# Two-model kernel, odd layer: retention beside the value and gate chunks, output rows by readiness, rotations in pairs, final norm by quarter

## The reference

```python
h = rms_norm_2(x, norm_g)
rq, rk, rv, rz, eq, ez = _split(h @ w_in, ODD_SPLITS)      # 1024, 1024, 2048, 2048, 256, 256 columns
q = apply_rotary(rq, rcos, rsin); k = apply_rotary(rk, rcos, rsin) * 256 ** -0.5     # 4 heads of 256
r_out = head_group_norm(retention(q, k, v))                # per head: (q k^T * decay) v, 512 wide, then (o - mean) / std
m_out = memory_attention(eq, mem_n, w_mem_kv)              # 4 heads of 64 over 256 memory rows
y = concatenate([r_out * silu(rz), m_out * silu(ez)]) @ w_out                        # 2304 rows
x = x + y
return rms_norm_2(x, final_norm_g)
```

## Time and profile before

| | |
|---|---|
| median of 3 runs | 2457.4 us |
| profiled execution | 2458.76 us |
| its span | 2456.9 us |
| TensorE busy | 2359.7 us (96%) |
| VectorE busy | 1742.9 us (71%) |
| ScalarE busy | 1350.2 us (55%) |
| mean granted TensorE clock | 0.987 |

### The profile page before, as it was taken

The page is one execution under the profiler, slowest core; times in us unless marked ns, Lnnn a source line. Parts: engine busy times, 40 slices in busy tenths (PEclk is TensorE's granted clock), DMA queues, the critical chain, the costliest instruction groups (busy, mean ns, idle before and its releaser), DMA issues.

```text
span 2456.9 us, 45173 instructions
## 1 busy us (share of the span) xinstructions
PE 2359.7 (96%) x15676; PEld 2112.0 (86%) x15676; DVE 1742.9 (71%) x3162; ACT 1350.2 (55%) x2520; POOL 42.0 (2%) x86
## 2 busy tenths in 40 slices
PE   8999999999999999899999999999999989998988
PEld 7889998999988888899999899988888867776866
DVE  4656998999755555675999899856556667765464
ACT  4545555777554545445444677645555536744533
POOL 1000000000000000000000000000000000000010
PEclk9999999999999999999999999999999999999999
DMA  6344555444566666455556444566665642344533
GB/s 227 121 143 151 179 171 163 147 139 144 170 193 195 190 194 191 145 179 173 179 170 174 144 143 143 170 194 190 212 187 176 190 122 83 95 159 138 159 110 120
DMA packets 136825, 397.45 MB, mean 162 GB/s; under 512 B 12304, under 2 KB 13520, under 8 KB 135920
## 3 DMA queue, kind: packets, MB, share of 16 engines
q1 hardware_dynamic: 134144, 384.97, 51.9%
q0 software_dynamic: 2544, 10.67, 1.3%
HBM read 394.54 MB, written 1.05 MB: 161 GB/s over the span
## 4 chain that ended last, share of the span: by engine, by line
PE 69%; DVE 24%; issue 4%; ACT 2%; POOL 0%; DMA 0%; DVEq 0%; ACTq 0%; POOLq 0%; SPq 0%
PE bank L968 28%; PE bank L952 14%; PE bank L838 11%; DVE wl L1582 8%; PE bank L844 7%; PE bank L981 4%; DVE arena L1786 1%; DVE arena L1787 1%; DVE arena L1789 1%; DVE arena L1788 1%; PE bank L905 1%; PE bank L893 1%; ACT wh L1233 1%; PE bank L878 1%; DVE arena L1785 1%
## 5 line engine op out<-in xcount | busy, mean ns | idle before, releaser
L1582 DVE TENSOR_TENSOR wl<-raw,wh 128x1024 fp32r<-128x1024 f32 (+1 forms) x732 | 893.8, 1222 | 516.1 <-ACT wh L1233 502.3
L1233 ACT ACTIVATE wh<-raw 128x1024 fp32r<-128x1024 f32 (+1 forms) x732 | 771.7, 1055 | 643.5 <-PE bank L968 340.1
L952 PE MATMUL bank<-xh,wh 128*128 128x256 f32 x2048 | 512.4, 288 | 0.0
L952 PE MATMUL bank<-xl,wh 128*128 128x256 f32 x2048 | 501.7, 283 | 0.0
L952 PEld LDWEIGHTS bank<-xh,wh 128*128 128x128 f32 x2048 | 392.0, 191 | 1.3 <-issue 0.2
L952 PEld LDWEIGHTS bank<-xl,wh 128*128 128x128 f32 x2048 | 392.8, 192 | 0.0
L952 PE MATMUL bank<-xh,wl 128*128 128x256 f32 x2048 | 293.2, 286 | 13.3 <-DVE wl L1582 13.3
L952 PEld LDWEIGHTS bank<-xh,wl 128*128 128x128 f32 x2048 | 262.8, 191 | 20.8 <-DVE wl L1582 19.2
L968 PE MATMUL bank<-wh,gl 128*128 128x512 f32 x1024 | 274.4, 390 | 1.7 <-DVE gl L1908 1.7
L968 PE MATMUL bank<-wh,gh 128*128 128x512 f32 x1024 | 274.1, 389 | 0.5 <-ACT gh L1391 0.5
L968 PE MATMUL bank<-wl,gh 128*128 128x512 f32 x1024 | 273.8, 389 | 0.0
(11 more groups left out here) (279 smaller groups left out, 2737.5 us busy)
## 6 DMA issues: line engine op xcount, KB each, us to landing
raw<-in_w_upT SPq DMA_DIRECT2D x256, 512.0 KB, 3.6
raw<-in_w_down SPq DMA_DIRECT2D x256, 512.0 KB, 4.3
raw<-in_l_w_in SPq DMA_DIRECT2D x84, 512.0 KB, 3.6
raw<-in_peer_w_query SPq DMA_DIRECT2D x32, 512.0 KB, 3.8
raw<-in_l_w_out SPq DMA_DIRECT2D x28, 512.0 KB, 3.7
raw<-in_attn_w_qkv SPq DMA_DIRECT2D x24, 512.0 KB, 4.3
raw<-in_conv_w_in SPq DMA_DIRECT2D x24, 512.0 KB, 3.8
arena<-in_na_bias POOLq DMA_DIRECT2D x4, 1024.0 KB, 5.9
```

The costliest lines, as they stand in the source:

```text
L952: last = pe.matmul(banks[b][:, 0:SEQ], lhsT=w[part][:, k, :], rhs=x_in[xp][:, k, :], start=(k == 0 and part == 0 and xp == 0), stop=(k == ...
L1233: act.activation(wh[:, n % SPLIT, 0:kts * cols], raw[:, n % RAW, 0:kts * cols], ACT.Copy)\
L1582: tt(wl[:, n % SPLIT, 0:kts * cols], raw[:, n % RAW, 0:kts * cols], wh[:, n % SPLIT, 0:kts * cols].bitcast(F32), ALU.subtract).then_inc(lo ...
```

## The change

The plan is rewritten. Rotations come in pairs, at (c, 3) and (c + 1, 0), and their transposes three units behind the second; the memory attention starts one unit later; a head's `ret_S` and `ret_O` follow when its value chunk is there, so they lie beside the chunks of values and gates. `ret_O` writes the normalised output over the values and no longer multiplies by the gate; a new kind `z` does that for both tiles when `silu` is done. The transposes of the gated output (`zT`) and their split (`z_low`) move into the plan, in the order `ODD_YT`, and the rows of `odd_out`'s weights follow that order; groups 6 and 7 come after the second unit of `odd_out`. The low half of the gated output gets a place of its own in the arena. In the last unit all products of the first bank come before those of the second, and VectorE is told between. ScalarE squares the first two quarters between the units of `odd_out`'s second half. Each quarter is multiplied by gain and sqrt(1024) into `final` as soon as it is added; the row scale is applied by VectorE to the first column half and by ScalarE to the second; the output goes out in four stores of 256 KB.

```diff
 ODD_PLAN = {
     (0, 0): [("turn", 2)],
-    (0, 3): [("rope", 0)], (1, 1): [("rope", 1)], (1, 2): [("odd_T", 0), ("odd_T", 1)],
-    (1, 3): [("rope", 2)], (2, 1): [("rope", 3)], (2, 2): [("odd_T", 2), ("odd_T", 3)],
-    (2, 3): [("rope", 4)], (3, 1): [("rope", 5)], (3, 2): [("odd_T", 4), ("odd_T", 5)],
-    (3, 3): [("rope", 6)], (4, 1): [("rope", 7)], (4, 2): [("odd_T", 6), ("odd_T", 7)],
-    (4, 3): [("silu", 4), ("odd_T", 8)],
-    (8, 1): [("ret_S", 0)],
-    (9, 3): [("silu", 0), ("ret_S", 1)], (10, 0): [("ret_O", 0)],
-    (10, 3): [("silu", 1), ("ret_S", 2)], (11, 0): [("ret_O", 1)],
-    (11, 3): [("silu", 2), ("ret_S", 3)], (12, 0): [("ret_O", 2)],
-    (12, 3): [("silu", 3), ("ret_O", 3)],
+    (0, 3): [("rope", 0)], (1, 0): [("rope", 1)], (1, 3): [("odd_T", 0), ("odd_T", 1), ("rope", 2)],
+    (2, 0): [("rope", 3)], (2, 3): [("odd_T", 2), ("odd_T", 3), ("rope", 4)],
+    (3, 0): [("rope", 5)], (3, 3): [("odd_T", 4), ("odd_T", 5), ("rope", 6)],
+    (4, 0): [("rope", 7)], (4, 3): [("odd_T", 6), ("odd_T", 7), ("silu", 4)],
+    (5, 0): [("odd_T", 8), ("ret_S", 0)],
+    (6, 1): [("ret_O", 0)], (6, 2): [("ret_S", 1)],
+    (7, 1): [("ret_O", 1)], (7, 2): [("ret_S", 2)], (7, 3): [("mem_z", 0)],
+    (8, 0): [("zT", 0)], (8, 1): [("ret_O", 2), ("z_low", 0)], (8, 2): [("ret_S", 3)],
+    (9, 1): [("ret_O", 3)], (9, 3): [("silu", 0)],
+    (10, 0): [("z", 0)], (10, 2): [("zT", 1), ("zT", 2)], (10, 3): [("z_low", 1), ("z_low", 2), ("silu", 1)],
+    (11, 0): [("z", 1)], (11, 2): [("zT", 3), ("zT", 4)], (11, 3): [("z_low", 3), ("z_low", 4), ("silu", 2)],
+    (12, 0): [("z", 2)], (12, 2): [("zT", 5), ("zT", 6)], (12, 3): [("z_low", 5), ("z_low", 6), ("silu", 3)],
+    (13, 0): [("z", 3), ("ahead", 2), ("z_low", 7), ("z_low", 8)],
 }
+ODD_YT = (8, 0, 1, 2, 3, 4, 5, 6, 7)
+ODD_LATE = {1: (7, 8)}
...
-    ODD_PLAN.setdefault((5 + _s // 4, _s % 4), []).append(("om", _s))
+    ODD_PLAN.setdefault((5 + (_s + 1) // 4, (_s + 1) % 4), []).append(("om", _s))
...
-        weight("odd_out", d["l1_w_out_2"], D)
+        weight("odd_out", d["l1_w_out_2"], D, rows=ODD_YT)
...
+            for n in range(2):
+                for ready, k in ((final_ready, n), (final_scaled, 2 + n)):
+                    c, t = k // 2, k % 2
+                    sp.wait_ge(ready, n + 1)
+                    sp.dma_start(out[t * P:(t + 1) * P, c * CHUNK:(c + 1) * CHUNK], final[:, t, c * CHUNK:(c + 1) * CHUNK])\
+                        .then_inc(stored_out, 16)
...
                 pool.wait_ge(ret_var, n + 1)
+                if n:
+                    pool.wait_ge(ret_scale, n)
...
+                        if by_bank and k0 + UKT == tiles:
+                            pe.wait_ge(hi_ready, n + 1)
+                            pe.wait_ge(lo_ready, n + 1)
+                            for b in range(2):
+                                for part, xp in ((0, 0), (0, 1), (1, 0)):
+                                    for kk in range(UKT):
+                                        last = pe.matmul(bank(js[b])[:, 0:cols], lhsT=lhs[xp][:, k0 + kk, b * P:(b + 1) * P],
+                                                         rhs=w[part][:, kk, :], start=False, stop=part == 1 and kk == UKT - 1,
+                                                         skip_group_check=True)
+                                if b == 0:
+                                    last.then_inc(first_bank, 1)
...
+            def odd_yT(k):
+                j, g = take("odd_yT", k), ODD_YT[k]
+                pe.wait_ge(y_ready, 5 if g == 8 else 6 + g // 2)
+                for q, src in enumerate(od_y_src[i][:, t, :] for i in (2 * g, 2 * g + 1) for t in range(TT)):
+                    last = pe.transpose(bank(j)[:, q * P:(q + 1) * P], src, ident[:])
+                done(last, j)
...
-            split_x("odd_yT", od_out, count_=9)
+            odd_steps(len(ODD_CHUNKS), 0)
+            highs(unit_of[J.of("odd_out", 0)])
+            for p in range(2):
+                squared_part("odd", p)
             highs(unit_of[J.of("odd_out", 3)])
-            norm(resid, updated("odd"))
+            for p in range(2, 4):
+                squared_part("odd", p)
+            act.wait_ge(row_scale, ROW_SCALES.index("final") + 1)
+            act.wait_ge(final_gained, 2)
+            for t in range(TT):
+                act.activation(final[:, t, CHUNK:D], final[:, t, CHUNK:D], ACT.Copy, scale=small[:, 6 + t:7 + t])\
+                    .then_inc(final_scaled, 1)
...
                     elif kind == "ret_O":
-                        dve.wait_ge(silu_done, 5 + k)
+                        js = [J.of("ret_O", TT * k + t) for t in range(TT)]
+                        for t in range(TT):
+                            wait_filled(dve, js[t])
+                            step(dve.bn_stats(bn[:, t], bank(js[t])[:, :]))
+                            tell(dve.bn_aggr(ret_stats[:, TT * k + t, :], bn[:, t]), ret_var, TT * k + t + 1)
                         for t in range(TT):
                             n = TT * k + t
...
                             dve.wait_ge(ret_scale, n + 1)
-                            o = view(E_TMP, RET_V)
-                            read_out(ts(o, bank(j)[:, :], ret_stats[:, n, 0:1], small[:, 30 + n:31 + n], ALU.subtract, ALU.mult), j)
-                            z = od_proj[:, t, ODD["rz"] + k * RET_V:ODD["rz"] + (k + 1) * RET_V]
-                            step(tt(z, z, o, ALU.mult))
+                            read_out(ts(ret_o(k, t), bank(js[t])[:, :], ret_stats[:, n, 0:1], small[:, 30 + n:31 + n],
+                                        ALU.subtract, ALU.mult), js[t])
+                    elif kind == "mem_z":
+                        tell(dve.nop(), y_ready, 5)
+                    elif kind == "z":
+                        dve.wait_ge(silu_done, 5 + k)
+                        z = od_proj[:, :, ODD["rz"] + k * RET_V:ODD["rz"] + (k + 1) * RET_V]
+                        o = od_proj[:, :, ODD["rv"] + k * RET_V:ODD["rv"] + (k + 1) * RET_V]
+                        tell(tt(z, z, o, ALU.mult), y_ready, 6 + k)
+                    elif kind == "z_low":
+                        split_low("odd_yT", od_out, 9, [k])
+                    elif kind == "ahead":
+                        lows(first_unit["odd_out"] + k)
...
             lows(unit_of[J.of("odd_out", 0)])
             add_quarters("odd_out", (0, 1))
+            for k in range(2):
+                step(gained(k))
             lows(unit_of[J.of("odd_out", 3)], 0)
-            add_quarters("odd_out", (2, 3))
+            dve.wait_ge(first_bank, 1)
+            r = resid[:, 0, CHUNK:D]
+            updated(tt(r, bank(J.of("odd_out", 2))[:, :], r, ALU.add))
+            add_quarters("odd_out", (3,))
+            for k in range(2, 4):
+                tell(gained(k), final_gained, k - 1)
             row_scales("final")
-            step(ts(small[:, 6:8], small[:, 6:8], math.sqrt(D), None, ALU.mult))
-            dve.wait_ge(extra_loaded["gain"], 32)
-            for k in range(4):
-                norm_rows(k, 6)
-            tell(dve.nop(), final_ready, 1)
+            for t in range(TT):
+                part = final[:, t, 0:CHUNK]
+                tell(ts(part, part, small[:, 6 + t:7 + t], None, ALU.mult), final_ready, t + 1)
```

More of the change, by code:

```diff
@@ L81 @@
 O_DECAY = 22016
-O_YT = O_ROPED
+O_YT, O_YT_LOW = O_ROPED, 25392
+assert O_YT + ODD_OUT // P * SEQ <= O_T + 2 * SEQ and O_YT_LOW + ODD_OUT // P * SEQ <= E_TMP
 UNIT = 1024
@@ L296, in build @@
         ev_out = parts("ev_out", E_YT, EVEN_OUT // P)
-        od_out = parts("od_out", O_YT, ODD_OUT // P)
+        od_out = [place(f"od_out_{p}", [P, ODD_OUT // P, SEQ], F32R, place_of["arena"] + 4 * words)
+                  for p, words in zip("hl", (O_YT, O_YT_LOW))]
         x_in = [xh, xl]
@@ L427, in add_jobs @@
                             J.add("norm_odd", 2, ring="other")
+                        elif kind == "zT":
+                            J.add("odd_yT", ring="other")
                         elif kind in ("even_T", "kvc", "cmp_S", "cmp_T", "cmp_O", "odd_T", "ret_S") or kind == "hid" and k == 0:
@@ L434, in build @@
         add_jobs("odd_in", len(ODD_CHUNKS), ODD_PLAN)
-        J.add("odd_yT", 9); J.add("odd_out", 4, own=False)
+        J.add("odd_out", 2, own=False, ring="projection")
+        J.add("odd_yT", 2, ring="other")
+        J.add("odd_out", 2, own=False, ring="projection")
         unit_of = {}
@@ L665, in _ @@
                     n += N_KEYS
[L666 to L669, removed]
+            for n in range(2):
[4 more added lines that the diff above has]
+                        .then_inc(stored_out, 16)
+            sp.wait_ge(stored_out, 16 * 4)
         @block.gpsimd
@@ L810, in norm_parts, with project @@
                 return lambda k0: split_ready(f"norm_{name}", 2 if k0 < 4 else 4)
-            def project(name, forms, lhs, tiles=KT, k=0, after=lambda u: None, ready=None):
```

(25 more changed lines are left out.)

24 lines of the change are left out of this document (16 added, 8 removed).

## The result

The changed kernel takes 2433.07 us (median of 4 runs, 2428.75 to 2433.41) against 2457.97 for the kernel before (4 runs beside it). The ratio is 0.9896, with a 95% interval of 0.9884 to 0.9909: 24.9 us, or 1.0%, faster. Forecast were 2431.7, within 2424 to 2441.

The account below looks back on a forecast made before the run. TensorE was taken as the bound where it has work, with the odd layer losing time only between units. 30.9 us removed less 5.2 added gave 25.7 net, so 2431.7 us, within 2424 to 2441.

Parts of the forecast that it names:

- (a): Rotations: four TensorE waits (8.2), one evacuation wait (2.6) and a half-clock unit's excess (1.7) go, 12.5 us.
- (i): First rotation pair: rotations and low halves back to back on VectorE make unit 7's low half 0.3 us late.
- (b): TensorE's waits for low halves of weights, made late by `ret_O` on VectorE: 3.3 us go.
- (c): Gap ahead of last projection: 15.4 us of waiting and 36 transposes become 4.3 between units, net 11.1 less.
- (d): Tail: fourth add (start a) 0.92 us earlier, end at a + 7.6 instead of a + 10.7; 4.0 us less.
- (h): Last projection: ScalarE squares two quarters before halving unit 63, making its high half late; 0.65 us added.
- (e): Chunk 6: TensorE's `ret_S` 1 waits for the bank of `ret_O` 0, which VectorE reads late; 2.1 us added.
- (f): ScalarE's bursts at (9, 3), (10, 3) and (11, 3) make high halves late; 0.5, 0.4 and 0.4, 1.3 us added.
- (g): Behind (12, 3), last output transposes wait for silu 3 and z 3; 0.8 us added.
- R1: Rival: VectorE becomes the bound in chunks 5 to 9, with waits at four `ret_O`; 2437.6 us, chance 0.12.
- R2: Rival: the new waits drop the clock; three dips add 5.1 us, 2436.8 us, chance 0.09.
- R3: Rival: the added waits do not appear, so 5.2 us come off; 2426.5 us, chance 0.12.

Follow-up runs that it names:

- e1: Kernel before with only the rotations, their transposes, the ninth transpose group and the memory attention moved: 2442.05 us, ratio 0.9937.
- e2: Kernel before with only the end changed (last unit by bank, `final` by quarter, four stores, squares between units): 2453.42 us, ratio 0.9985.
- e6: Changed kernel, but behind unit 25 VectorE makes the low half and takes `ret_O` 0 before waiting for the attention output: 2427.15 us, ratio 0.9878.
- e7: Changed kernel with ScalarE's work in chunks 9 to 12 spread differently (silu 0 later, transposes' splits behind silu's unit): 2428.31 us, ratio 0.9881.
- e8: Kernel before with only the gated output's low half moved to the changed kernel's place, word 25392: one run, odd layer 261.0 us against 260.1.
- e5: Changed kernel with rotations and their transposes (groups 0 to 7) back at the old places: 2441.87 us, ratio 0.9933.
- e3: Changed kernel with all nine groups of output transposes and their splits behind the last chunk: 2436.18 us, ratio 0.9909.
- e4: Changed kernel with five edits: the new orders of VectorE at (6, 1) and ScalarE in chunks 9-12, later squares, later last low-half wait: 2426.29 us, ratio 0.9871.
- e11: Changed kernel with old places of rotations and transposes in chunks 2 to 4, first pair as changed: one run, odd layer 241.3 us against 234.7.

## Why the prediction was right, point by point

In the odd layer 25.7 us net were forecast and 25.4 measured. Term by term:

| term | forecast | measured | from |
|---|---|---|---|
| (a) less (i), rotations | 12.2 | 13.3 | e1 |
| (b), (c) low halves, gap | 14.4 | 15.1 | the rest of the sum |
| (d) less (h), tail | 3.35 | 2.7 | e2 |
| (e) bank wait | -2.1 | -2.0 | e6 |
| (f), (g) bursts, z 3 | -2.1 | -2.6 | e7 |
| last unit's low half | 0 | -0.2 | e7 |
| place of the low half | 0 | -0.9 | e8 |
| sum | 25.7 | 25.4 | |

The sum agrees by construction, since (b) and (c) are its rest. The starts of the units give them once more: unit 56 starts 10.2 us earlier in the changed kernel than in e1, and with the 2.0, 2.6 and 0.2 that (e), (f), (g) and the place of the low half cost up to there it is 15.0. That the net came out within 0.3 us is in part luck: the terms were 1.9 us short on one side and 2.3 on the other.

(a) The mechanism holds, the size was 1.1 short. Idle rows of 2.06 and 2.6 us were taken as the whole wait. By the starts of the units, e1 gains 2.28 us at the second and at the third of the four waits and 5.0 at the fourth and the evacuation together. With 2.28 for the first as well, that is 11.9 and 1.1 more than the 10.8 taken. What is left of the first pair, the half-clock unit less (i), is 1.2 and not 1.4. The output transposes ahead of the last projection, at half clock for most of their time in both kernels, took 6.63 us in e1 and 6.93 before, another 0.3, which no edit of e1 accounts for. The half clock was counted as one of four by chance; the traces before and of e2, e5 and e8 show it at the same wait each time. Whether the executions without a trace do the same is not shown.

(i) The low half of unit 7 is late, as forecast: its products start at 2212.74, where 2212.45 was their turn, 0.3 us.

(b) and (c) were not measured alone. e3 shows that (c) was two things: of the gap, moving retention takes away VectorE's chain, and moving the transposes gains a further 4.5 us. How much of the 15.1 is (b) and how much is the first part of (c) was not separated. That the transposes cost little beyond their own time in the plan is seen in the changed kernel's waits, which hold one for them.

(d) was mis-sized by 0.65 us, since the end came at a + 8.25 and not at a + 7.6. The 4.47 us from the first issue to the end lie above the 4.34 that two larger stores took and that were to be the upper bound; issuing four took 1.82 us where two took 0.83, and the end came 2.67 behind the last issue, where 2.3 were taken. VectorE's tensor_scalar out of SBUF is 0.49 us, not 0.69: here the Trainium skill (VectorE: DVE Perf Modes, The perf-mode tier table) was right against the nearest rows. It gained nothing, because the row scale came later: VectorE starts with it at 2426.61 = a + 3.26, not at a + 2.93. One step of GpSimd's (L709, 128x2) takes 0.55 us where it took 0.23 (L689). The prediction had put the products with the gain beside it at no cost. The step takes 0.23 in e1 and e8, which keep the old tail, and 0.54 to 0.55 in e2 and e5, which have the new one. Whether VectorE's products are what slows it is not shown.

(e), (f), (g), (h) each appeared at its place, with its releaser: 1.80 us, then 0.48, 0.17 and 0.17, then 0.79, and 0.24 in the second half of the last projection.

One sentence was wrong: "High is wanted when unit i + 2 starts (5.44 with nothing between)". Unit i + 2 starts 2.72 us behind the end of unit i; 5.44 is the turn of the half that is made one step later, and the sums of (f) to (h) used it for that one. But it made the last unit look safe. That unit waits for its low half before its first matmul; the low half is done 2.6 us behind the end of unit i by the prediction's own times, 0.1 ahead of that, and 0.3 of lateness was enough to cost the 0.24 us of the changed kernel, which the sum lacked.

Also lacking was the place of the low half, 0.9 us, which the prediction did not look at.

R1, R2 and R4 are refuted for this kernel: TensorE waits for VectorE only once in chunks 5 to 9, and the clock stays at full through the odd layer. R3 did not come: e4 shows what it would have given.

## What to carry to other kernels

Work on other engines hides beside a stream of matmuls only if each engine takes it as it becomes ready and in the order in which TensorE will ask for it: of the 5.5 us that the changed kernel still lost, 2.0 were VectorE sitting out a wait while ready work lay behind it, and 3.1 were ScalarE doing work that was not yet wanted ahead of what TensorE would ask for next. To find this ahead of a run, write down for each step when a buffer is filled, when it is read and when its ring comes round to it, with the start-to-start times of the trace and not its idle times. And a gap that holds a wait and a run of small matmuls is worth splitting, since the matmuls behind the wait can run at half clock: behind 8.2 us of waiting, the 36 transposes of the kernel before took 6.7 us, 4.7 us of that at a granted clock of 0.50, against 3.8 by the pace of those between units.

## What the runs showed of the hardware

The start of the low half of the stationary tiles in SBUF changes the pace of the matmuls. With word 25392 of the arena a unit of 12 matmuls takes 2.77 us, with 25408 and 25600 (and 17920 in the kernel before) 2.72: 1.8% of the last projection, 0.9 us. All eight traces with the first place have 2.77 and all five with another 2.72. The good ones lie multiples of 256 bytes from the high half and 25392 does not (48320 bytes, 64 beyond a multiple of 128). Which of the alignments between 64 and 256 bytes is enough was not tried, nor whether it is the distance to the high half that counts or the place itself, since only the low half was moved. Why it costs time is not shown.

Four waits of the same 2.06 us in a row, and the granted clock falls to half behind the first alone, in four of four traces (before, e2, e5, e8); with the first wait gone, the other three leave it at full (e11). The Trainium skill (TensorE: Matmul & The Clock Gate, Part 1) ties the fall to idling and has the moment at which the clock changes vary from run to run; here idling of this length was not enough by itself, and the fall came at the same wait in all four. All that precedes this wait is nearly the same in the four, so they show one situation four times; what makes the first wait differ from the others stays open.
